# Suffix sums and scores of a second attention as high and low products, and an earlier solve at the start of a recurrence

## The reference, cut to what matters

```python
# stick breaking, 8 heads of 128; scale = 128 ** -0.5
z = jnp.einsum('bhqd,bhkd->bhqk', qb, kb) * scale
log_keep = jnp.where(causal, jax.nn.log_sigmoid(-z), 0.0)
later = lax.cumsum(log_keep, axis=3, reverse=True) - log_keep
weights = jnp.where(causal, jnp.exp(jax.nn.log_sigmoid(z) + later), 0.0)
out = jnp.einsum('bhqk,bhkd->bhqd', weights, vb)
# WKV-7, one step a token
sa = jnp.einsum('bhvk,bhk->bhv', state, -kk_t)
state = state * w_t + sa[..., None] * (kk_t * a_t) + v_t[..., None] * k_t
out_t = jnp.einsum('bhvk,bhk->bhv', state, r_t)
```

## Time and profile before

| | before |
|---|---|
| median of 3 runs | 3511.78 us (3511.09 to 3512.23) |
| profiled execution | 3503.65 us, span 3501.8 us |
| TensorE busy | 3374.8 us, 96% of the span |
| VectorE, ScalarE, GpSimd busy | 50%, 39%, 12% |
| chain that ended last | TensorE 86%, VectorE 3%, DMA 3%, GpSimd's queue 3% |
| mean granted TensorE clock | 0.989 |
| second attention, scores of head 0 to the last head | 1370 to 1762 us |
| recurrence | about 2869 to 3290 us |

### The profile page before, as it was taken

One profiled execution on the slowest core, in us unless ns is written; L12 is line 12 of the kernel. 1 busy time (PEld: TensorE's weight loads), 2 busy tenths in 40 slices (PEclk: granted clock), 3 DMA queues, 4 the chain that ended last, 5 costly groups with the idle time before them and its releaser, 6 DMA issues.

```text
span 3501.8 us, 51377 instructions
## 1 busy us (share of the span) xinstructions
PE 3374.8 (96%) x20948; PEld 2660.2 (76%) x20948; DVE 1766.1 (50%) x2313; ACT 1372.6 (39%) x1584; POOL 410.0 (12%) x718
## 2 busy tenths in 40 slices
PE   7899999999999999999999998999999999899897
PEld 1566888887887887887788876888888867677685
DVE  5745666665656433334323348242424237778545
ACT  1323344343334223334323227141414147777423
POOL 0000222322122000000000000000000014444000
PEclk9999999999999999999999999999999999999998
DMA  9522232323332442222232323333333333333322
GB/s 346 183 78 76 102 102 90 108 99 102 99 108 90 147 148 85 72 96 72 73 101 90 110 96 116 120 120 120 121 122 122 123 111 80 83 71 78 127 96 72
DMA packets 178956, 381.46 MB, mean 109 GB/s; under 512 B 111728, under 2 KB 117104, under 8 KB 145008
## 3 DMA queue, kind: packets, MB, share of 16 engines
q1 hardware_dynamic: 164352, 326.73, 28.5%
q0 software_dynamic: 14448, 52.50, 4.4%
HBM read 342.49 MB, written 35.13 MB: 108 GB/s over the span
## 4 chain that ended last, share of the span: by engine, by line
PE 86%; DVE 3%; DMA 3%; POOLq 3%; SPq 2%; issue 1%; ACT 1%; DVEq 0%; POOL 0%; ACTq 0%
PE PJ L291 19%; PE PJ L293 18%; PE PJ L292 18%; PE AB L291 6%; PE AB L293 6%; PE AB L292 6%; POOLq L1532 1%; POOLq L1529 1%; PE AB L230 1%; DMA WK<-ada 1%; DMA X<-blocks_scratch 1%; PE AB L658 1%; PE AB L1167 1%; PE AB L1627 1%; PE AB L440 1%
## 5 line engine op out<-in xcount | busy, mean ns | idle before, releaser
L291 PE MATMUL PJ<-XH,WH 128*128 128x512 f32 x2848 | 1131.9, 397 | 17.2 <-DVE XL L414 10.3
L293 PE MATMUL PJ<-XH,WL 128*128 128x512 f32 x2848 | 1112.3, 391 | 0.0
L292 PE MATMUL PJ<-XL,WH 128*128 128x512 f32 x2848 | 1111.4, 390 | 0.0
L322 DVE TENSOR_TENSOR WL<-RAW,WH 128x2048 fp32r<-128x2048 f32 (+2 forms) x239 | 545.0, 2281 | 658.7 <-ACT WH L317 653.3
L317 ACT ACTIVATE WH<-RAW 128x2048 fp32r<-128x2048 f32 (+2 forms) x240 | 453.4, 1889 | 848.5 <-PE PJ L293 589.2
L291 PEld LDWEIGHTS PJ<-XH,WH 128*128 128x128 f32 x2848 | 536.1, 188 | 144.0 <-issue 31.7
L293 PEld LDWEIGHTS PJ<-XH,WL 128*128 128x128 f32 x2848 | 535.7, 188 | 112.7
L292 PEld LDWEIGHTS PJ<-XL,WH 128*128 128x128 f32 x2848 | 536.4, 188 | 110.7 <-issue 3.8
L291 PE MATMUL AB<-XH,WH 128*128 128x512 f32 (+1 forms) x960 | 381.1, 397 | 10.2 <-DVE XL L414 7.7
L293 PE MATMUL AB<-XH,WL 128*128 128x512 f32 (+1 forms) x960 | 375.4, 391 | 0.0
L292 PE MATMUL AB<-XL,WH 128*128 128x512 f32 (+1 forms) x960 | 375.2, 391 | 0.0
(11 more groups left out here) (417 smaller groups left out, 3733.7 us busy)
## 6 DMA issues: line engine op xcount, KB each, us to landing
RAW<-w SPq DMA_DIRECT2D x232, 1024.0 KB, 4.9
WK<-ada SPq DMA_DIRECT2D x32, 1024.0 KB, 5.4
GATE<-gate POOLq DMA_DIRECT2D x64, 256.0 KB, 3.1
rkvg_scratch<-WK POOLq DMA_DIRECT2D x16, 1024.0 KB, 4.8
x_scratch<-X POOLq DMA_DIRECT2D x8, 1024.0 KB, 6.1
X<-rkvg_scratch SPq DMA_DIRECT2D x32, 256.0 KB, 3.5
RAW<-rkvg_scratch SPq DMA_DIRECT2D x32, 256.0 KB, 3.5
X<-xT SPq DMA_DIRECT2D x4, 1024.0 KB, 15.7
```

Source lines behind the costliest of these rows:

```text
L291: nc.tensor.matmul(bank[0:width, n, :], hi, xh, start=first, stop=False)
L292: nc.tensor.matmul(bank[0:width, n, :], hi, xl, start=False, stop=False)
L293: m = nc.tensor.matmul(bank[0:width, n, :], lo, xh, start=False, stop=last)
L322: nc.vector.tensor_tensor(WL[k % 2][:, :, 0:w], narrow(RAW[k % 2], w), WH[k % 2][:, :, 0:w].bitcast(F32), ALU.subtract).then_inc(wl_ready, 1)
```

## The change

In the second attention, q and k are rounded to float32r by ScalarE (QK_HI) and their remainders made by VectorE (QK_LO); the scores are three float32r products for each block in place of one float32 product. The softplus values and the sums of later blocks get high and low parts in the same way (SP_HI, SP_LO, LATER_HI, LATER_LO); the suffix sums are two products for each float32 one, since the matrices of -1 are exact in float32r (MATR, copied once at the start). `sp` now counts twice a head, `log` and `gs` too. The suffix products move from the end of slot 2 to `between`, after tile 1 of slot 3. ScalarE and VectorE split slot 3's weights ahead of steps(1) instead of ahead of steps(2) (`pull`).

In the recurrence, GpSimd solves pair 0 before the memsets and not after them; the zeroing of the DRAM scratch is done earlier, from a buffer of zeros of its own (ZEROS); SyncE sends the solutions out and back ahead of sp_levels(0). Pair 0's bt products go from bank 6 to bank 2 (BT_BANK), into the last slot of the last group; the operations of pair 1 that followed in rounds -3 and -2 (rate, growth, decay_before on ScalarE; key, ke, re of pair 0, rate_key and d on VectorE) go ahead of that group's evacuation, into first_act and first_dve.

The core of the diff (act_group changes as dve_group does; the calls in wv_act and wv_dve of what has moved start one pair later):

```diff
-                      ahead=2, split_first=False):
+                      ahead=2, split_first=False, pull=False):
             for k in range(SLOTS):
-                if ahead - 1 <= k < SLOTS - 1:
+                if ahead - 1 <= k < SLOTS - 1 and not (pull and k == 2):
                     split(act, G, k + 1)
-                elif k == SLOTS - 1 and not last:
+                if pull and k == 1:
+                    split(act, G, 3)
+                if k == SLOTS - 1 and not last:
                     next_split(act, G + 1, 0)
...
             wait(act, s("mix_done"), BASE + h)
             nc.scalar.activation(wk(16), wk(3), ACT.Silu).then_inc(sk("gs"), 1)
+            act.drain()
+            nc.scalar.activation(QK_HI, wk(0, 2), ACT.Copy).then_inc(sk("gs"), 1)
...
+                ql, kl = QK_LO[:, 0:SEQ], QK_LO[:, SEQ:2 * SEQ]
+                qh, kh = QK_HI[:, 0:SEQ], QK_HI[:, SEQ:2 * SEQ]
                 for kb in range(TB):
-                    m = nc.tensor.matmul(AB[:, kb, kb * P:SEQ], wk(1)[:, kb * P:(kb + 1) * P], wk(0)[:, kb * P:SEQ],
-                                         start=True, stop=True)
+                    at, z = slice(kb * P, (kb + 1) * P), AB[:, kb, kb * P:SEQ]
+                    nc.tensor.matmul(z, kh[:, at], qh[:, kb * P:], start=True, stop=False)
+                    nc.tensor.matmul(z, kh[:, at], ql[:, kb * P:], start=False, stop=False)
+                    m = nc.tensor.matmul(z, kl[:, at], qh[:, kb * P:], start=False, stop=True)
                 m.then_inc(sk("zt"), 1)
-            elif k == 2:
-                wait(pe, sk("sp"), h + 1)
+            elif k == "later":
+                wait(pe, sk("sp"), 2 * h + 2)
                 for kb in range(TB):
                     more = kb < TB - 1
-                    m = nc.tensor.matmul(AB[:, kb, kb * P:SEQ], mat("neg_suffix"), PK(10, kb), start=True,
-                                         stop=not more)
+                    z, at = AB[:, kb, kb * P:SEQ], slice(COL_O[kb], COL_O[kb] + COL_W[kb])
+                    nc.tensor.matmul(z, NEG_SUFFIX, SP_HI[:, at], start=True, stop=False)
+                    m = nc.tensor.matmul(z, NEG_SUFFIX, SP_LO[:, at], start=False, stop=not more)
                     if more:
-                        m = nc.tensor.matmul(AB[:, kb, (kb + 1) * P:SEQ], mat("neg_ones"), later_sum(kb),
-                                             start=False, stop=True)
+                        z = AB[:, kb, (kb + 1) * P:SEQ]
+                        nc.tensor.matmul(z, NEG_ONES, LATER_HI[kb], start=False, stop=False)
+                        m = nc.tensor.matmul(z, NEG_ONES, LATER_LO[kb], start=False, stop=True)
                 m.then_inc(sk("later"), 1)
...
                 nc.scalar.activation(a, a, ACT.Ln, bias=SC[:, 3:4]).then_inc(sk("log"), 1)
+                wait(act, sk("sp"), 2 * h + 1)
+                nc.scalar.activation(SP_HI, WK[:, 10 * SEQ:10 * SEQ + CAUSAL], ACT.Copy).then_inc(sk("log"), 1)
...
+                wait(dve, sk("gs"), 2 * h + 2)
+                nc.vector.tensor_tensor(QK_LO, wk(0, 2), QK_HI.bitcast(F32), ALU.subtract)
                 nc.vector.tensor_copy(wk(15), AB[:, 0, :]).then_inc(sk("v"), 1)
...
-                dve.drain()
+                dve.drain().then_inc(sk("sp"), 1)
                 nc.vector.tensor_tensor(later_sum(1)[:, P:2 * P], PK(10, 2)[:, P:2 * P], PK(10, 3), ALU.add)
                 nc.vector.tensor_copy(later_sum(1)[:, 0:P], PK(10, 2)[:, 0:P])
                 dve.drain()
                 nc.vector.tensor_tensor(later_sum(0)[:, P:3 * P], PK(10, 1)[:, P:3 * P], later_sum(1), ALU.add)
                 nc.vector.tensor_copy(later_sum(0)[:, 0:P], PK(10, 1)[:, 0:P])
-                dve.drain().then_inc(sk("sp"), 1)
+                dve.drain()
+                for kb in range(2):
+                    nc.vector.tensor_copy(LATER_HI[kb], later_sum(kb))
+                dve.drain()
+                for kb in range(2):
+                    nc.vector.tensor_tensor(LATER_LO[kb], later_sum(kb), LATER_HI[kb].bitcast(F32), ALU.subtract)
+                wait(dve, sk("log"), 2 * h + 2)
+                nc.vector.tensor_tensor(SP_LO, sp, SP_HI.bitcast(F32), ALU.subtract).then_inc(sk("sp"), 1)
...
+            if q == 1:
+                pe.wait_ge(wv("masked"), 3)
             pe_pairs(pe, q, T_D, 2, wv("nt"))
 
         def pe_bt(pe, q):
-            pe_pairs(pe, q, T_E, 6, wv("bt"))
+            if q == 0:
+                pe.wait_ge(wv("sig"), sig_done(1))
+            pe_pairs(pe, q, T_E, BT_BANK(q), wv("bt"))
...
+            elif n == 2:
+                pe_bt(pe, 0)
...
-            at(t + 2, lambda p: pe_bt(pe, p))
+            at(t + 2, lambda p: pe_bt(pe, p), 1)
...
+                act_rate(act, 1)
+                act_growth(act, 1)
+                act_decay_before(act, 1)
...
+                dve_key(dve, 1)
+                dve_ke(dve, 0)
+                dve_re(dve, 0)
+                dve_rate_key(dve, 1)
+                dve_d(dve, 1)
...
+            sp.wait_ge(wv("y_zero"), 1)
+            for v in range(2):
+                for r in range(2):
+                    sp.dma_start(by_row(y_d[v], r), ZEROS[rows(r)].rearrange("p (z i) -> p z i", i=CH)
+                                 ).then_inc(wv("zeroed"), 16)
             sp.wait_ge(wl_ready, SLOTS * G_OUT3 - 1)
             sp_load(sp, 1)
             sp_load_lora(sp, 1)
             sp_blocks_out(sp, 0)
             sp_blocks_in(sp, 0)
-            sp.wait_ge(wv("y_zero"), 1)
-            for v in range(2):
-                for r in range(2):
-                    sp.dma_start(by_row(y_d[v], r), YT(0)[rows(r)].rearrange("p (z i) -> p z i", i=CH)
-                                 ).then_inc(wv("zeroed"), 16)
-            sp_levels(sp, 0)
             sp.wait_ge(wv("zeroed"), 64)
             sp_solved_out(sp, 0)
+            sp.wait_ge(wv("y_zero"), 2)
             sp_solved_back(sp, 0)
+            sp_levels(sp, 0)
...
-                if n == 15:
+                if n == 14:
+                    nc.gpsimd.memset(ZEROS[:, :], 0.0)
+                    nc.gpsimd.drain().then_inc(wv("y_zero"), 1)
+                elif n == 15:
+                    pool_solve(pool, 0)
                     pool.wait_ge(wl_ready, SLOTS * G_OUT3 - 1)
                     pool.wait_ge(slot_done, SLOTS * G_OUT3 - 1)
-                    nc.gpsimd.memset(YT(0), 0.0)
                     nc.gpsimd.memset(ws(T_N5, 2), 0.0)
                     nc.gpsimd.drain().then_inc(wv("y_zero"), 1)
-                    pool_solve(pool, 0)
...
-                pe_group(pe, G_EVA + h, steps=lambda k: sb_pe(pe, h - 1, k))
-            pe_group(pe, G_POOL, steps=lambda k: sb_pe(pe, HEADS - 1, k))
+                pe_group(pe, G_EVA + h, steps=lambda k: sb_pe(pe, h - 1, k),
+                         between=lambda n, m: n == 1 and sb_pe(pe, h - 1, "later"))
+            pe_group(pe, G_POOL, steps=lambda k: sb_pe(pe, HEADS - 1, k),
+                     between=lambda n, m: n == 1 and sb_pe(pe, HEADS - 1, "later"))
...
+            nc.vector.tensor_copy(NEG_SUFFIX, mat("neg_suffix"))
+            nc.vector.tensor_copy(NEG_ONES, mat("neg_ones"))
```

More of the change, by code:

```diff
@@ L135, in build @@
         RAW = [sb(f"RAW{r}", [P, SKT * GC]) for r in range(2)]
+        WK_AT = (2 * KT + 4 * SKT + KT + 2 * SKT) * SEQ
         NWK = 18
+        TBL_AT = WK_AT + NWK * SEQ
         WK = sb("WK", [P, NWK * SEQ])
@@ L149, in build @@
         GATE = [sb(f"GATE{r}", [P, SEQ]) for r in range(2)]
+        MATR = sb("MATR", [P, 2 * P], F32R)
+        ZEROS = sb("ZEROS", [P, SEQ])
         PJ = ctx.enter_context(nc.psum_tensor("PJ", [P, 4, SEQ], F32))
@@ L378, in dve_group @@
         def dve_group(dve, G, evac, steps=None, pre=None, last=False, split=dve_split, next_split=dve_split, by_tile=False, early=False,
-                      ahead=2, split_first=False):
+                      ahead=2, split_first=False, pull=False):
             for k in range(SLOTS):
-                if ahead - 1 <= k < SLOTS - 1:
+                if ahead - 1 <= k < SLOTS - 1 and not (pull and k == 2):
                     split(dve, G, k + 1)
-                elif k == SLOTS - 1 and not last:
+                if pull and k == 1:
+                    split(dve, G, 3)
+                if k == SLOTS - 1 and not last:
                     next_split(dve, G + 1, 0)
@@ L1146, in build @@
         BASE = 2 * HEADS
+        SPLIT_HI = placed("SPLIT_HI", [P, 3 * SEQ], TBL_AT + CAUSAL + SEQ)
+        SB_LO = placed("SB_LO", [P, 16 * SEQ], WK_AT)
+        QK_HI, QK_LO = SPLIT_HI[:, 0:2 * SEQ], SB_LO[:, 0:2 * SEQ]
+        SP_HI, SP_LO = SPLIT_HI[:, 0:CAUSAL], SB_LO[:, 10 * SEQ:10 * SEQ + CAUSAL]
+        LATER_HI = (SB_LO[:, 14 * SEQ + P:15 * SEQ], SPLIT_HI[:, CAUSAL:CAUSAL + 2 * P], SP_HI[:, COL_O[3]:CAUSAL])
+        LATER_LO = (SB_LO[:, 13 * SEQ:13 * SEQ + COL_W[1]], SB_LO[:, 13 * SEQ + COL_W[1]:13 * SEQ + COL_W[1] + COL_W[2]],
+                    SP_LO[:, COL_O[3]:CAUSAL])
```

(27 more changed lines are left out.)

9 lines of the change are left out of this document (3 added, 6 removed).

## The result

The changed kernel takes 3517.78 us (median of 9 runs, 3513.42 to 3524.79), the kernel before in the same comparison 3508.55 us (9 runs, 3502.12 to 3512.23). The ratio is 1.0027, with a 95% interval of 1.0017 to 1.0036: the change costs 9.2 us, 6 to 12.6. The forecast was +3.0 us.

What follows compares the result with a forecast made beforehand. TensorE, busy 96% of the span, and the recurrence where it waits were taken as the bound; +2.5 us (attention) and +0.5 us (recurrence) made +3.0 us, a median near 3514.8 us, range 3505 to 3522.

Steps and rivals of the forecast that it cites:

- The saving: Second attention: score and suffix products on TensorE take 3.97 us instead of 5.73, saving 1.76 us a head.
- The rival with narrow products at fp32's price: Second attention: seven narrow fp32r products cost what fp32 does, 0.81 us more a head, 3521 us; chance 0.2.
- The operands: Slot 3 of the second attention: suffix products' inputs are ready before TensorE arrives, with 0.9 us left, so no wait.
- S: Start of a head's score products in the second attention, from which the forecast counts times in us.
- The stall: End of each second-attention group: TensorE waits 2.07 us a head for VectorE's copy of the projections out of PSUM.
- E: End of a head's suffix sums in the second attention, from which the forecast counts times in us.
- The rival without a stall: Second attention: VectorE's copy is ready in time, leaving only the saving of 14 us, 3498 us; chance 0.12.
- part 1: Second attention's products in high and low parts, with suffix products moved: net +2.5 us over eight heads.
- part 2: Recurrence's start reordered: pair 0 solved sooner, nothing gained; +0.5 us, from -2 to +1.5.
- The step about what holds the load: Recurrence's start: pair 2's load also waits for VectorE's gs of pair 0, so is issued at most 0.3 us sooner.
- the collision: Recurrence's start: GpSimd's 1 MB store now lies beside pair 2's load; priced 0 to 1.5 us, taken as 0.8.
- The rival that it holds: Recurrence's start: the clock does not fall, 2.5 us less, 3512 us with the stall; chance 0.15.

Runs made afterwards that it cites:

- the kernel with the split moved: Changed kernel, but ScalarE and VectorE split the next group's slot 0 before the work awaiting the suffix products; 3496.32 us, 0.9964 of the kernel before.

## Why the prediction was right, and where it was wrong

**The saving.** Forecast 1.90 us for the scores and 2.07 for the suffix sums; the rows have 1532.17 - 1530.31 = 1.86 and 2.04. The scores' last three products and the projections behind them, in TensorE's timeline:

```profile
1531.89 0.22 PE L1181 MATMUL AB<-SPLIT_HI 128*128 128x128 f32 x1
1531.94 0.28 PE L1182 MATMUL AB<-SB_LO,SPLIT_HI 128*128 128x128 f32 x1
1532.06 0.27 PE L1183 MATMUL AB<-SPLIT_HI,SB_LO 128*128 128x128 f32 x1
1532.17 0.44 PE L295 MATMUL PJ<-XH,WH 128*128 128x512 f32 x1
1532.45 0.40 PE L296 MATMUL PJ<-XL,WH 128*128 128x512 f32 x1
```

A 128-column product behind another takes 0.11 us, the value taken from the two weight loads; the first of a group of them takes 0.05 to 0.07. The product behind the narrow ones takes 0.28 us in place of 0.23; the sum counts such a delay, 0.1 us, for float32 only. Twice 0.05 us a head belong to the new products too, and 5.73 - 1.86 - 2.04 - 0.1 = 1.73 us is what was measured (1.72). The rival with narrow products at fp32's price is out. The figure of the Trainium skill (TensorE: Matmul & The Clock Gate, Back-to-back issue gap), 81 ns for such a product, lies between the two; the sum by it would have been 0.2 us a head too good.

**The operands.** Forecast S + 17.4 against TensorE at S + 18.3. Measured from S = 1369.99: the 1280-column subtraction ends at 1386.58, S + 16.6, and TensorE comes at S + 18.25. The two casts of 384 and 256 columns took 0.36 and 0.28 us, less than the bound of 0.56 and 0.42.

**The stall.** Forecast: the copy ends at E + 9.63, TensorE arrives at E + 7.63 and goes on at E + 9.7. Measured from E = 1390.28: the copy ends at 1399.74, E + 9.46, and TensorE goes on at 1399.97, E + 9.69. The rival without a stall is out; the kernel with the split moved shows that its price, 14 us, was right too (12 to 15 measured in three kernels).

**The step that failed** stands in the sum of part 1, 8 x (2.07 - 1.76) = +2.5 us. Its terms were off by little: measured 8 x (2.14 - 1.72) = +3.4. What is missing is a term: a stall of 2 us of TensorE was priced at its own length, while three of the eight stalls in one trace, five in another and three in a third took 1.6 us more, through the clock. That is +4.8 to +8 us, in the changed kernel's trace +4.8. The forecast speaks of the clock only at the recurrence's start, where TensorE idles for 5.14 us and where it weighed the clock as a gain. It did not ask the same of the idle time that it created itself. The Trainium skill (TensorE: Matmul & The Clock Gate, What's actually happening), which the forecast named there, has idleness throttle the array; the rows at 1450 agree, those at 1558 show that the same idle time can also pass without it. Saving, stall, fall and part 2 make 3.4 + 4.8 + 0.6 = 8.8 us, beside 9.2 measured, but with the recurrence varying by 10 us from one execution to the next, that they meet so well is partly luck.

**Part 2.** The step about what holds the load was right. In the changed kernel the solve's results go out 8.84 us after the bonus of pair 0 in place of 16.5, 7.7 us sooner (forecast 5.6), and the load of pair 2 at 21.67 in place of 22.12 and, in the three other traces with the old code, 22.44, 22.55 and 22.72: 0.4 to 1.0 sooner (forecast at most 0.3). The chain of waits, to be laid beside the earlier trace rows, and GpSimd's store:

```profile
2882.62 5.29 DMA X<-rkvg_scratch
...
2888.70 2.08 PE AB L1584 x2
2890.78 1.90 PE PJ L1649 x32
```

```profile
2879.55 0.81 POOL L2305 DMA_DIRECT2D rkvg_scratch<-WK  x1 [11.15 <-DVE WK L1379]
```

The landing takes 5.29 us where it took 4.13. But 4.13 is the shortest of the four traces with the old code (4.13 to 4.85, mean 4.48), where the store goes out over 4 us ahead of the load; in the six with the new code, where it goes out 0.9 us ahead, the landing takes 5.28 to 5.41 (mean 5.33). That is 0.85 us more, where the forecast took 0.8 for the collision. The nt products of pair 2 come at 50.3 and 51.0 to 51.1 us after the bonus in four traces with the old code (mean 50.9), at 51.35 to 51.65 in five with the new (mean 51.5): +0.65 us, forecast +0.5. No run changed the store alone, so that the collision is the cause of the slower landing is argued and not shown: in the six traces SyncE's four issues of the load together also take 3.0 us in place of 2.0. nt of pair 1 came 1.7 us sooner (forecast 1.5) and was worth nothing.

**The clock at the recurrence's start.** The rival that it holds is out. The idle time ahead of the chain's products is there as before, 5.07 us in place of 5.14, only in front of a later product, and the clock is low around it (table by stage, timeline of TensorE):

```profile
2877.00:2887.00 10.00, 3.22 (x40) 2.56 (x40) 7.51 (x12) 1.44 (x3) 2.21 (x3) 0.65 0.64 206
```

```profile
2888.70 2.08 PE L1584 MATMUL AB<-X,MAT 128*128 128x512 f32 x2 [5.07 <-ACT X L1820]
```

The key sum and r1 took 2.08 and 1.90 us, as in the earlier trace rows.

**The level.** The forecast of the median, 3514.8 us, started from 3511.78, the median of the first three runs of before. Over the 9 runs beside the changed kernel, these three among them, it is 3508.55, and in two later comparisons 3508.76 (23 runs) and 3506.29 (29 runs). The time of 3517.78 us lies within the forecast's range, whose upper part had been given to narrow products at a higher price and was filled by the fall of the clock, but measured against its own neighbour the change costs three times what was forecast, and lands on the slower side of 0.2%, to which the prediction gave 0.22.

## What to carry to other kernels

When a product is moved to a later place, look at what follows its result on the other engines and where those must be done next: here 1.72 us were saved on TensorE, the 2.81 us that VectorE had spare ahead of an evacuation copy were used up, and TensorE stalled for 2.14 us. Queue work that waits for nothing (the split of the next weights) ahead of work that waits. And price an idle time of TensorE that a change creates from its own length up to its length and a clock fall (here 1.6 us).

## What the runs showed of the hardware

An idle time of about 1.9 us in a stream that is otherwise without a gap was enough to let the granted clock fall behind three, five and three of the eight stalls of three traces (to 0.53 to 0.75 over the next three us); each fall cost 1.6 us, and with eight products in the gap there was none behind 16 gaps of two traces. What decides between the heads is open: idle time and work around it are the same in the rows.

Ten executions of the recurrence took 435.3 to 448.8 us; two of the same code that were in step at its start ended it 10.2 us apart. Half of that arose where one landing took 5.18 us and the clock stood at 0.61 to 0.71 over the next ten us; the other half was not followed up. Where a recurrence runs through DRAM like this, an effect under 5 us has to be read from the trace of its own stretch.
